# Two layers of a streaming encoder on one core: a couple's raw weights in one transfer instead of two

## The reference

```python
for l in range(DEPTH):            # DEPTH = 2
    ...                           # attention branches, merge, output projection
    h = rmsnorm(x, g_ffn[l])
    x = x + (jax.nn.silu(h @ w_gate[l]) * (h @ w_up[l])) @ w_down[l]
```

## Time and profile before

| | |
|---|---|
| time, median of 3 (lowest, highest) | 1811.33 us (1810.67, 1811.88) |
| profiled execution | 1809.71 us, of which the profile spans 1807.9 us |
| TensorE busy | 1765.7 us, 98% of the span |
| VectorE, ScalarE, GpSimd busy | 56%, 39%, 35% |
| granted TensorE clock | 0.997 of full speed |
| transfers of couple weights | 72 of 512 KB, 3.5 us median from issue to landing |

### The profile page before, as it was taken

One profiled execution on the slowest core, in us unless ns is written; L12 is line 12 of the kernel. 1 busy time (PEld: TensorE's weight loads), 2 busy tenths in 40 slices (PEclk: granted clock), 3 DMA queues, 4 the chain that ended last, 5 costly groups with the idle time before them and its releaser, 6 DMA issues.

```text
span 1807.9 us, 31587 instructions
## 1 busy us (share of the span) xinstructions
PE 1765.7 (98%) x12122; PEld 1693.0 (94%) x12122; DVE 1021.1 (56%) x1602; ACT 703.7 (39%) x1401; POOL 631.5 (35%) x515
## 2 busy tenths in 40 slices
PE   7999999999999999999999999999999999999997
PEld 7988887999999999999999888789999999999997
DVE  5563445474683655747546444456658655747463
ACT  5254345313442433434432634543234333434343
POOL 1422321144134454544333232113430444544433
PEclk9999999999999999999999999999999999999998
DMA  5233523342223131321222235143422231322312
GB/s 172 83 114 108 149 76 100 129 168 70 71 80 103 52 115 49 105 82 62 78 83 70 84 114 135 65 138 128 140 70 71 79 108 47 105 82 65 99 53 88
DMA packets 63791, 171.30 MB, mean 95 GB/s; under 512 B 8120, under 2 KB 13912, under 8 KB 63512
## 3 DMA queue, kind: packets, MB, share of 16 engines
q1 hardware_dynamic: 62808, 167.73, 28.6%
q10 hardware_dynamic: 864, 1.97, 0.3%
HBM read 151.03 MB, written 19.43 MB: 94 GB/s over the span
## 4 chain that ended last, share of the span: by engine, by line
PE 92%; ACT 3%; DVE 3%; POOL 1%; issue 1%; DMA 0%; POOLq 0%; DVEq 0%; ACTq 0%
PE acc L1521 38%; PE acc L1360 12%; PE acc L1598 11%; PE psU L1598 9%; PE acc L1553 4%; PE psS L1598 3%; PE acc L1467 1%; PE psU L1311 1%; PE psU L1325 1%; PE acc L1452 1%; PE acc L1290 1%; PE psU L1340 1%; POOL w_lo L704 1%; PE acc L1680 1%; PE acc L1695 1%
## 5 line engine op out<-in xcount | busy, mean ns | idle before, releaser
L704 POOL TENSOR_TENSOR w_lo<-w_raw,w_hi 128x512 fp32r<-128x512 f32 x204 | 274.0, 1364 | 649.9 <-ACT w_hi L768 649.9
L768 ACT ACTIVATE w_hi<-w_raw 128x1024 fp32r<-128x1024 f32 (+2 forms) x194 | 173.9, 898 | 429.0 <-PE acc L1521 378.0
L714 POOL TENSOR_TENSOR w_lo<-w_raw,w_hi 128x256 fp32r<-128x256 f32 (+1 forms) x160 | 132.4, 848 | 239.8 <-ACT w_hi L768 239.8
L733 POOL TENSOR_TENSOR s_raw<-w_raw 128x512 f32<-128x512 f32 x72 | 106.7, 1482 | 246.7 <-DVE s_lo L1993 108.7
L2343 DVE TENSOR_TENSOR xT<-acc,xT 128x640 f32<-128x640 f32 x88 | 72.6, 825 | 198.7 <-PE acc L1521 164.7
L788 ACT ACTIVATE s_hi<-s_raw 128x512 fp32r<-128x512 f32 x144 | 90.2, 626 | 139.9 <-POOL s_raw L733 53.3
L1360 PE MATMUL acc<-h_hi,w_hi 128*128 128x320 f32 x512 | 137.8, 350 | 1.2 <-DVE gate L1973 1.2
L1993 DVE TENSOR_TENSOR s_lo<-s_raw,s_hi 128x512 fp32r<-128x512 f32 x144 | 114.3, 808 | 41.7 <-ACT s_hi L788 41.5
L1993 DVE TENSOR_TENSOR a_lo<-w_raw,a_hi 128x512 fp32r<-128x512 f32 x108 | 117.5, 1088 | 23.2 <-ACT a_hi L788 22.8
L1521 PE MATMUL acc<-h_hi,w_hi 128*128 128x320 f32 x512 | 118.5, 313 | 2.0 <-POOL w_lo L704 2.0
L1521 PE MATMUL acc<-act_hi,w_hi 128*128 128x320 f32 x518 | 118.6, 310 | 1.0 <-POOL w_lo L714 1.0
(11 more groups left out here) (348 smaller groups left out, 4830.5 us busy)
## 6 DMA issues: line engine op xcount, KB each, us to landing
w_raw<-in_w SPq DMA_DIRECT2D x116, 512.0 KB, 3.5
w_raw<-in_w_pairs SPq DMA_DIRECT2D x72, 512.0 KB, 3.5
w_raw<-in_w SPq DMA_DIRECT2D x48, 256.0 KB, 2.6
gates<-gate SPq DMA_DIRECT2D x32, 320.0 KB, 2.2
tmp<-gates SPq DMA_DIRECT2D x32, 320.0 KB, 3.3
w_raw<-in_w SPq DMA_DIRECT2D x32, 320.0 KB, 2.8
cb_t<-in_cb_t SPq DMA_DIRECT2D x16, 256.0 KB, 3.1
cb_v<-in_cb_v SPq DMA_DIRECT2D x16, 256.0 KB, 2.8
```

Source lines behind the costliest of these rows:

```text
L704: ins = pool.tensor_tensor(w_lo[:, s, a:b], w_raw[:, s, a:b], w_hi[:, s, a:b], ALU.subtract)
L714: ins = pool.tensor_tensor(w_lo[:, n % 2, a:b], w_raw[:, n % 2, a:b], w_hi[:, n % 2, a:b], ALU.subtract)
L733: pool.tensor_tensor(part_raw[o][:, :], x, y, op).then_inc(s_sum, 1)
L768: act.activation(w_hi[:, slot, 0:cols], w_raw[:, slot, 0:cols], ACT.Copy).then_inc(s_w_hi, 1)
```

## The change

Both halves of a couple come in one transfer of `[128, 2048]` f32 (1 MB), and each of the two raw buffers has one semaphore instead of one per half. The waits ahead of the one transfer are the later of those ahead of the two: for couple 0 and behind a turn both slots of `w_raw` must be converted (`plain` units instead of `plain - 1` and then `plain`), for other couples both `pair_converted` conditions hold before it. GpSimd's sums wait for the one semaphore. ScalarE's A11 and A12, which read half 0 alone, wait for the whole transfer.

```diff
-        pair_loaded = [[sem(f"pair_loaded{r}{n}") for n in range(2)] for r in range(2)]
+        pair_loaded = [sem(f"pair_loaded{r}") for r in range(2)]
...
-            def load_pair(l, i, unit):
+            def load_pair(l, i):
...
-                sp.dma_start(raw[r][:, unit, :], io["w_pairs"][l * PAIRS + i][:, unit, :]).then_inc(pair_loaded[r][unit], 16)
+                sp.dma_start(raw[r][:, :, :], io["w_pairs"][l * PAIRS + i]).then_inc(pair_loaded[r], 16)
...
-                    for u in range(2):
-                        if i == 0 or (i > 1 and turn_of(i - 1) is not None):
-                            sp.wait_ge(s_w_hi, l * UNITS + (plain - 1 + u))
-                            sp.wait_ge(s_w_lo, l * UNITS + (plain - 1 + u))
-                        elif i == 1:
-                            sp.wait_ge(acc_full, l * TILES + TILE_DOWN)
-                        else:
+                    if i == 0 or (i > 1 and turn_of(i - 1) is not None):
+                        sp.wait_ge(s_w_hi, l * UNITS + plain)
+                        sp.wait_ge(s_w_lo, l * UNITS + plain)
+                    elif i == 1:
+                        sp.wait_ge(acc_full, l * TILES + TILE_DOWN)
+                    else:
+                        for u in range(2):
                             pair_converted(l * PAIRS + i - 2, u)
-                        load_pair(l, i, u)
+                    load_pair(l, i)
...
-                for u in range(2):
-                    pool.wait_ge(pair_loaded[raw_of(i)][u], 16 * RAW_USE[now])
+                pool.wait_ge(pair_loaded[raw_of(i)], 16 * RAW_USE[now])
...
-                    unit = raw_part[o][0]
-                    act.wait_ge(pair_loaded[raw_of(i)][unit], 16 * RAW_USE[now])
+                    act.wait_ge(pair_loaded[raw_of(i)], 16 * RAW_USE[now])
```

## The result

| | before | changed |
|---|---|---|
| median of 5 (lowest, highest) | 1811.88 us (1810.67, 1812.79) | 1822.0 us (1819.62, 1822.89) |
| ratio to before | 1 | 1.0059, 95% interval 1.0048 to 1.0069 |
| the same two, measured again beside the last experiments | 1811.63 us | 1822.31 us, 1.0054 (1.0040 to 1.0068) |
| profiled execution, its span | 1809.71, 1807.9 us | 1822.0, 1820.2 us |

The account below looks back on a forecast made before the run. TensorE, busy 98% of the span, was taken to bound the kernel. Layer starts 5.4 us plus turns 2.4 us made 7.8 us, 1817.5 on the profiled execution, forecast as 1819.1 us (range 1813.5 to 1825).

Parts of the forecast that it names:

- Which places: Two layer starts and six turns of four blocks lose time; two turns of five blocks and ordinary couples lose nothing.
- The transfer's time: One 1 MB load lands 4.5 us after its issue, an estimate between bounds of 3.2 and 6.4 us.
- slow transfer rival: A 1 MB load takes 6.2 us, moving 8 places by 1.7 us more each: 1832.7 us; chance 6%.
- Start of a layer, up to S2: Couple 0: ScalarE stands on A11, first product starts at 522.5, S2 at 524.85, 2.1 us later.
- Start, couple 1: Layer start: couple 1's A11 ends 3.0 us later, a 0.3 us wait goes; net 2.7 us per layer.
- Turn, first wait: Behind six turns of four blocks, A22 of the couple before waits for the add of four: 0.4 us each.
- Turn, second wait: After a turn's first wait: the next wait has over 1 us and nothing is given back; no further loss forecast.
- The sum: Layer starts 5.4 us plus turns 2.4 us make 7.8 us over the kernel before; forecast 1819.1 us.
- benign order: VectorE wins the port each time: starts cost 1.2 to 1.8 us per layer, turns nothing; 1814.3 us; chance 20%.
- faster rival: GpSimd's first add for couple 1 begins behind its A11 low part: 1.9 us per layer gained, 1807.5 us; chance 4%.

Follow-up runs that it names:

- run 3: Changed kernel with couple 0 and the 8 couples behind turns in two halves again, the other 26 in one transfer; 1809.0 us, 0.999.
- run 6: Changed kernel with VectorE doing the add of four ahead of the next couple's S2 low part; 1813.67 us, 1.0021.
- run 8: Kernel before, add of four ahead of S2's low part, GpSimd's sums of couple 1 held until VectorE has its A11 low part; 1808.6 us, 0.9989.
- run 7: Kernel before with VectorE doing the add of four ahead of the next couple's S2 low part; 1808.63 us, 0.9989.
- run 4: Changed kernel, but couple 0 and couples behind turns come in two halves, both issued only when both slots are free; 1821.28 us, 1.0049.
- run 5: Kernel before, its two transfers issued as there, but ScalarE's conversions of raw parts wait for both halves; 1812.59 us, 1.0011.
- run 9: Changed kernel, couple 0 and couples behind turns in halves, add of four ahead of S2's low part; 1808.45 us, 0.9983.
- run 11: The changed kernel itself measured again, nothing edited, against the kernel before; 1822.31 us, 1.0054.

## Why the prediction was right, point by point

- **Which places.** Right. Starts and turns of four blocks pay; the turn of five blocks and the ordinary couples don't (5.17 to 5.30; run 3).
- **The transfer's time.** 4.5 us estimated; 4.7 to 4.9 measured at couple 0 and at the couples behind turns, the places that pay. The slow transfer rival falls there. The eight transfers issued 0.5 us behind another of 1 MB, those of the odd couples at turns, took 6.7 to 8.1 us, and no engine waited for one of them. The Trainium skill's table (DMA: Bandwidth & Descriptors, section "Measured (HBM→SBUF, 128 partitions, SWDGE, issued from GpSimd)") with 6.15 us for 1 MB is for another kind of queue, and is not borne out for a lone transfer on this one; the page's fit, 4.4 us, is near.
- **Start of a layer, up to S2.** Right to a tenth of a us, steps between included: first product predicted at 522.5, S2 at 524.85; measured, corrected, 522.50 and 524.87.
- **Start, couple 1.** This term was too large: 2.7 us forecast per layer, 2.0 measured. The step "They now lie across one VectorE subtraction more, 0.9 us" was right (act_lo takes 1.79 us now), but the last subtraction, A11's, is stretched no longer: 0.68 us at 536.11, since GpSimd's fourth add waited until 536.27 for the S4 low part. I had kept all three stretched, so A11 of couple 1 came 2.0 us later and not 3.0. The 0.3 us that I let go away behind that product stayed, because the S2 low part ahead of the add still took 1.76 us.
- **Turn, first wait.** Right in kind and nearly in size: 0.4 us forecast, 0.5 to 0.6 measured with the weight load that the wait also holds.
- **Turn, second wait.** This failed. I wrote "the next wait has over 1 us, and nothing is given back"; the next couple's A22 loses as much again, at all six turns. The premise was wrong in the kernel before already: the add at the turn has 1.3 us of room, the next one only 0.2 us (671.01 to 671.21), and no row that I had put on record shows it. It is the same add one couple on, at the end of a chain on VectorE and ScalarE that starts from S4's low part, and that took 1.70 us at 671.05 where it had taken 1.05. Why the phase of GpSimd's adds had moved there is argued from the rows (its sums start later by the first wait); that the add's place carries the wait is shown by run 6. The term was 2.4 us and measured 6.6; at 1.1 us a turn it lies over the upper bound of 1.0 that I gave it.
- **The sum.** 5.4 + 2.4 = 7.8 against 4.0 + 6.6 = 10.6. One term too large by 1.4, the other too small by 4.2. The total was in range with its shares the wrong way round, and the two errors offset each other in part: that the forecast came within 3 us is partly luck.
- **Rivals.** The benign order would give no waits at turns; there are twelve. The faster rival needed GpSimd's sums behind A11's low part; run 8 made exactly that, and even then the gain was 0.4 us per layer over run 7, not 1.9.

## What to carry to other kernels

Two transfers that feed one tile from two slots freed at different times are not the same as one: the joint transfer starts with the later slot, and every in-order engine that needed the first part alone now stands still with all that is queued behind it. Look for the cost in what stands behind the stalled operation, not in the operation; here it was a gate tile and an add that were not waiting for these weights. Read the room of every product that comes by, not of the first alone. And when one wait appears in a repeating pattern, follow the disturbance through the next round before calling it over; it may be lost twice.

## What the runs showed of the hardware that was not expected

- A 1 MB load (128 partitions of 8 KB) landed 4.7 to 4.9 us after its issue in 27 of the 36 places and 5.2 us in one, against 3.2 to 3.3 for 512 KB and 4.9 us for two halves issued back to back (run 4: first issue at 654.62; GpSimd's first add follows at 659.67). Eight that were issued 0.5 us behind another 1 MB load took 6.7 to 8.1 us.
- TensorE's clock is at the lower level for some us in one place or another of an execution: 299 to 307 us in the profiled run of the changed kernel (0.60), near the end in that of the kernel before (0.70). The first cost about 3 us, and so did one near 1195 us in the traces of runs 5, 7, 9 and 11: as much as the effects looked for here. Only rows next to each other could tell them apart.
- The exclusion between VectorE's subtractions of two SBUF tiles and GpSimd's adds showed as whole operations: 0.69 us alone, 1.7 to 1.8 us when they alternate (1.0 to 1.4 where they overlap in part). Where the two start close together the first keeps its time: VectorE at 516.43 took 0.69 us and GpSimd at 516.47 took 1.81. Operations that read PSUM kept their time in the trace before, 0.48 us for 128x320 and 0.82 for 128x640, with GpSimd running or not. Run 8 shows it from the other side.
